# A third buffer for raw weights, and a begin that runs two units side by side on halves of weights, in a fused decoder-layer kernel

## The chip, the cores and the metric

The kernel runs on one core of a Trainium2 chip. The metric is the device time of one launch in microseconds. It is 1373.68 us as the median of three runs (1371.19 to 1373.77).

## The reference, cut to what matters

One inference step of a hybrid decoder layer: 2048 prompt tokens and 32 sample tokens (8 sequences of 4), width 1024, all in float32.

```
h = rmsnorm(x) * norm_g                 # per token
z = h @ w_in                            # 1024 -> 5120: q, f, i, g_a, u, g_b, m_a, m_b
o, S = gated linear recurrence(silu(q), 1 - fgate, i, log fgate), 4 heads of 128, chunks of 32
y_a = (rmsnorm(o) * silu(g_a)) @ w_proj_a
y_b = (group mix(causal means of 2/4/8/16 of u) * scale * silu(g_b)) @ w_proj_b
out = x + (sigmoid(m_a) * y_a + sigmoid(m_b) * y_b) @ w_out
y = rmsnorm(out) * final_norm_g         # outputs: y, the states of both branches
```

## The kernel before, in words

The 2080 tokens are cut into 5 tiles of 416. In each tile the kernel goes through 56 units of weights in a fixed order (`UNITS`): four heads of f, q, i, g; four pairs u, b; the gates ma, mb and the projections y; and eight "out" units. A unit is a 128 x 1024 block of weights, 512 KB, loaded again in every tile. In this text "unit 4" is the fifth, the f of the second head.

Every product is done in three parts for precision. A weight block arrives raw in `wraw`; ScalarE copies it to a rounded high part `whi` (`split`, L807); VectorE subtracts to get the rest, `wlo` (L1061); the input has parts `hhi` and `hlo` likewise. TensorE then does whi x hhi, whi x hlo and wlo x hhi for each of 8 blocks of 128 rows, 24 products a unit (L535 to L537), summed in one of four PSUM banks `Z`. Unit n uses bank n mod 4 as long as no y unit has come, so unit 4 has to wait (`opened`) until the bank of unit 0 has been read.

There are `RAW` = 2 raw buffers and `RING` = 4 buffers for the parts. SyncE loads unit s + 2 at its slot s, once VectorE has made the low part of unit s (L432). ScalarE splits unit s + 3 at its slot s.

Every engine has its own instruction list, written out by hand and worked through in order; they meet by semaphores. Only semaphores and the order within a list set the order of the work.

The begin is special. The input of the first tile isn't normalised before the products: the kernel multiplies with x * norm_g and scales each result afterwards by 1/rms (`xrs0`), in `scale` on VectorE (L1495, L1489). For that, ScalarE squares the 8 blocks (`square`, L1026), VectorE adds them in six steps to two sums (L1530), TensorE adds over partitions with two products of full float32 with ones (`x_squares`, L790), and ScalarE takes logarithm and exponential (`x_norm`, L821, `x_norm_exp`, L825). The ScalarE list does x_norm after the splits of units 3, 4 and 5. TensorE begins with four warm-up products on constant data (`WARM`, L795, two passes each), then `first_unit` (unit 0, in the order in which blocks of the input come), then `late_low` for units 1 and 2 (both products with whi first, those with wlo last; x_squares stands inside unit 2), then the regular units.

After the g of a head (slot 4) VectorE runs that head's chain: decay sums (L1101), factors, keys (L1152), the transpose of the keys to `kt` (L1145, L1147), the split of the next unit and more. SyncE stores `kt` to memory (L497) and reads it back transposed as `ktm` (L506, L508). TensorE takes `ktm` ahead of unit 8 (L591): what stands behind L591 in its list, thus the rest of the kernel, waits for it.

Of the kernel before, what the change touches and what calls it, by code (L numbers as in the profile page):

```python
# [19 lines left out]
F32 = mybir.dt.float32  # L20
# [22 lines left out]
RAW = 2  # L43
# [3 lines left out]
WARM = 4  # L47
# [71 lines left out]
def step_kernel(nc, xT, w_all, consts, w_pool, s_in, buf_in, yT, sp_out, pp_out, ss_out, ps_out):  # L119
    with ExitStack() as ctx:  # L120
# [22 lines left out]
        wraw = [put(f"wraw{i}", [D]) for i in range(RAW)]  # L143
# [78 lines left out]
        vms_at = region(2 * 4 * 4 * P)  # L222
        vms = [put(f"vms{i}", [4, P], F32R, vms_at + 4 * 4 * P * i) for i in range(2)]
        xrs0 = put("xrs0", [T], F32, vms_at)
# [70 lines left out]
        lbe_made = sem("lbe_made")  # L295

# [72 lines left out]
        def raw(t, n):  # L369

            return wraw0[n - RAW] if first(t) and RAW <= n < EARLY else wraw[n % RAW]

        def raw_landed(engine, t, n):
# [3 lines left out]
            elif first(t) and n < EARLY:  # L377
                engine.wait_ge(w0_landed[n - RAW], 16)
            else:
                engine.wait_ge(w_landed[n % RAW], 16 * (t * (NU // RAW) + n // RAW))  # L380
# [23 lines left out]
        def _(sp):  # L404
            for i in range(4):
                sp.dma_start(xin[:, 2 * i:2 * i + 2, :], xT[0, :, 2 * i:2 * i + 2, :]).then_inc(x0_landed[i], 16)
                if i == 0:
                    sp.dma_start(cst[:], consts).then_inc(cst_landed, 16)
                if i == 0:
                    sp.dma_start(wraw[0][:], w_all[0]).then_inc(w_landed[0], 16)  # L410
            sp.dma_start(wraw[1][:], w_all[1]).then_inc(w_landed[1], 16)
# [3 lines left out]
            for n in range(EARLY, FIRST):  # L415
                sp.wait_ge(wlo_made, n - EARLY + 1)
                sp.dma_start(wraw[n % RAW][:], w_all[n]).then_inc(w_landed[n % RAW], 16)
            def tile(t, last):
                for s in range(NU):
# [9 lines left out]
                    if (n < NU or not last) and not (first(t) and n < FIRST):  # L429

                        sp.wait_ge(wlo_made, nth(t, NU, s))
                        sp.dma_start(wraw[n % RAW][:], w_all[n % NU]).then_inc(w_landed[n % RAW], 16)  # L432
# [25 lines left out]
                    if s == 32:  # L458
# [4 lines left out]
                        sp.dma_start(xres[:], xT[t]).then_inc(xres_landed, 16)  # L463
# [67 lines left out]
        def _(pe):  # L531
# [179 lines left out]
            def tile(t, last):  # L711
                for s, (kind, i) in enumerate(UNITS):
# [3 lines left out]
                    if first(t) and s < 3:  # L716
                        if s == 0:
                            first_unit()
                        else:
# [32 lines left out]
            def first_unit():  # L752

                out = Z[0][:, 0:T]
                pe.wait_ge(whi_made, 1)
                for k in range(KD):
                    c = slice(k * P, (k + 1) * P)
                    pe.wait_ge(hhi_made, k + 1)
                    pe.matmul(out, whi[0][:, c], hhi[k][:], start=(k == 0), stop=False)
                    pe.wait_ge(hlo_made, k + 1)  # L760
                    pe.matmul(out, whi[0][:, c], hlo[k][:], start=False, stop=False)
                    if k:
                        first_low(out, k - 1, False)
                first_low(out, KD - 1, True).then_inc(acc_done, 1)

            def late_low(u):
# [3 lines left out]
                for k in range(KD):  # L770
                    if u == 2 and k == 3:
# [9 lines left out]
            def first_low(out, k, final):  # L781
# [947 lines left out]
```

## Time and profile before

| | |
|---|---|
| three runs, median (lowest, highest) | 1373.68 us (1371.19, 1373.77) |
| profiled execution, its own time | 1373.4 us |
| its span, first to last instruction | 1371.7 us |
| TensorE busy | 1358.3 us, 99% of the span |
| VectorE, ScalarE, GpSimdE busy | 933.3, 682.7, 231.2 us |
| mean granted TensorE clock | 0.998 |

The profile is one execution. PE is TensorE's matmul, PEld its weight load, DVE is VectorE, ACT ScalarE, POOL GpSimdE and SPq the queue in which SyncE issues DMAs. Times are counted from the start of the span. A matmul's duration is longer than the step to the next one, as matmuls are pipelined: the step between two starts is what one costs.

### The profile page before, as it was taken

Reading aid. Unit: us, or ns where it says so; the run is one execution under the profiler, and the core shown is the slowest. Engines: PE = TensorE matmul, PEld = TensorE weight load, DVE = VectorE, ACT = ScalarE, POOL = GpSimd, SP = SyncE. Lnnn points to the kernel's source line nnn. Section 1 sums busy time; section 2 is a strip of 40 time slices with the busy share of each in tenths; the row PEclk is TensorE's granted clock in tenths of the full one; section 3 lists DMA queues with packets and bytes.
Section 4 is the critical chain, followed back from the end, with each engine's and each line's share of the span. In section 5 each row is a group of like instructions: output and inputs, shape, how many; then the busy total and the mean of one; then the engine's idle time right before and its main releaser. Section 6 shows DMA issues by size and latency. Waiting matters only on the chain.

```text
span 1371.7 us, 21201 instructions
## 1 busy us (share of the span) xinstructions
PE 1358.3 (99%) x8254; PEld 1342.2 (98%) x8254; DVE 933.3 (68%) x1608; ACT 682.7 (50%) x986; POOL 231.2 (17%) x210
## 2 busy tenths in 40 slices
PE   9999999999999999999999999999999999999997
PEld 7999999999999999999999999999999999999997
DVE  7899555668995456689944566898445589964443
ACT  6565444354674344556633445666334556653332
POOL 2003121120131211101312111012220200130001
PEclk9999999999999999999999999999999999999999
DMA  6544533246545333465363334554533476535329
GB/s 202 145 131 127 208 123 122 94 130 182 135 134 212 119 123 108 132 190 136 109 222 108 123 108 142 170 148 134 195 117 100 137 177 200 178 109 172 119 98 95
DMA packets 140260, 195.92 MB, mean 143 GB/s; under 512 B 83712, under 2 KB 100480, under 8 KB 138496
## 3 DMA queue, kind: packets, MB, share of 16 engines
q1 hardware_dynamic: 140160, 194.56, 47.2%
q8 instruction: 66, 1.08, 0.4%
q14 instruction: 34, 0.28, 0.1%
HBM read 174.91 MB, written 19.61 MB: 142 GB/s over the span
## 4 chain that ended last, share of the span: by engine, by line
PE 81%; DVE 11%; DMA 3%; issue 2%; ACT 2%; SPq 1%; DVEq 0%; ACTq 0%
PE Z L535 25%; PE Z L537 25%; PE Z L536 25%; DVE wlo L1061 2%; DMA wraw<-w_all 1%; DVE h_b L1101 1%; PE B L591 1%; PE B L679 1%; PE B L669 1%; DVE kj L1152 1%; DVE xres L1457 1%; DVE h_d L1111 0%; DVE s_all L1193 0%; DMA xin<-xT 0%; ACT whi L807 0%
## 5 line engine op out<-in xcount | busy, mean ns | idle before, releaser
L1061 DVE TENSOR_TENSOR wlo<-wraw,whi 128x1024 fp32r<-128x1024 f32 x280 | 373.6, 1335 | 308.0 <-ACT whi L807 307.8
L535 PE MATMUL Z<-hhi,whi 128*128 128x416 f32 x1576 | 552.6, 351 | 0.0
L537 PE MATMUL Z<-hhi,wlo 128*128 128x416 f32 x1576 | 549.4, 349 | 0.0
L536 PE MATMUL Z<-hlo,whi 128*128 128x416 f32 x1576 | 549.3, 349 | 0.0
L807 ACT ACTIVATE whi<-wraw 128x1024 fp32r<-128x1024 f32 x280 | 295.6, 1056 | 426.7 <-PE Z L537 336.5
L535 PEld LDWEIGHTS Z<-hhi,whi 128*128 128x128 f32 x1576 | 296.0, 188 | 0.9 <-issue 0.6
L536 PEld LDWEIGHTS Z<-hlo,whi 128*128 128x128 f32 x1576 | 296.0, 188 | 0.5
L537 PEld LDWEIGHTS Z<-hhi,wlo 128*128 128x128 f32 x1576 | 295.8, 188 | 0.2
L537 PE MATMUL Z<-mhi,wlo 128*128 128x416 f32 x320 | 112.3, 351 | 0.0
L536 PE MATMUL Z<-mlo,whi 128*128 128x416 f32 x320 | 111.9, 350 | 0.0
L535 PE MATMUL Z<-mhi,whi 128*128 128x416 f32 x320 | 111.5, 348 | 0.0
L536 PE MATMUL Z<-ylo,whi 128*128 128x416 f32 x320 | 111.4, 348 | 0.0
L537 PE MATMUL Z<-yhi,wlo 128*128 128x416 f32 x320 | 111.4, 348 | 0.0
L535 PE MATMUL Z<-yhi,whi 128*128 128x416 f32 x320 | 111.4, 348 | 0.0
L1619 POOL TENSOR_TENSOR mA<-mA,mB 128x416 f32<-128x416 f32 x40 | 43.5, 1088 | 341.1 <-DVE mB L1264 341.1
L1590 POOL TENSOR_TENSOR pa<-ext 128x430 f32<-128x430 f32 (+1 forms) x20 | 28.0, 1400 | 307.0 <-DVE ext L1493 98.0
L1564 POOL TENSOR_TENSOR yacc<-yacc,ysq 128x416 f32<-128x416 f32 x34 | 37.0, 1088 | 158.4 <-ACT ysq L1014 158.4
L1264 DVE TENSOR_TENSOR mB<-Z,gB 128x416 f32<-128x416 f32 x40 | 23.7, 592 | 58.6 <-PE Z L537 58.3
L1558 POOL TENSOR_TENSOR xacc<-xacc,xsq 128x416 f32<-128x416 f32 x28 | 42.2, 1509 | 113.7 <-ACT xsq L815 113.7
L536 PEld LDWEIGHTS Z<-mlo,whi 128*128 128x128 f32 x320 | 60.1, 188 | 0.6
L535 PEld LDWEIGHTS Z<-mhi,whi 128*128 128x128 f32 x320 | 60.1, 188 | 0.1
L537 PEld LDWEIGHTS Z<-mhi,wlo 128*128 128x128 f32 x320 | 60.1, 188 | 0.0
(249 smaller groups left out, 1613.1 us busy)
## 6 DMA issues: line engine op xcount, KB each, us to landing
wraw<-w_all SPq DMA_DIRECT2D x280, 512.0 KB, 3.5
xres<-xT SPq DMA_DIRECT2D x5, 1664.0 KB, 7.1
xin<-xT SPq DMA_DIRECT2D x4, 1664.0 KB, 7.9
yT<-xres SPq DMA_DIRECT2D x4, 1664.0 KB, 8.5
v_blocks<-h_vt SPq DMA_DIRECT2D x80, 52.0 KB, 3.1
vtm<-v_blocks SPq DMA_DIRECT2D x20, 192.0 KB, 4.0
ktm<-k_blocks SPq DMA_DIRECT2D x20, 192.0 KB, 3.6
k_blocks<-kt SPq DMA_DIRECT2D x64, 52.0 KB, 1.9
```

The source lines that it names most:

```text
L535: pe.matmul(out, wh, xh, start=first, stop=False)
L536: pe.matmul(out, wh, xl, start=False, stop=False)
L537: return pe.matmul(out, wl, xh, start=False, stop=final)
L591: mm = pe.matmul(B6[:, g * P:(g + 1) * P], ktm[:, g, :], vtm[:, g, :], start=True, stop=True)
L669: pe.matmul(B5[:, c], vtm[:, g, :], at_sb[:, c], start=(g == 0), stop=False, skip_group_check=True)
L807: act.activation(whi[n % RING][:], raw(t, n)[:], ACT.Copy).then_inc(whi_made, 1)
L1061: dve.tensor_tensor(wlo[n % RING][:], raw(t, n)[:], whi[n % RING][:].bitcast(F32), ALU.subtract).then_inc(wlo_made, 1)
L1264: dve.tensor_tensor(out[j % 2][:], z_bank(acc, j)[:, 0:T], gate[j % 3][:], ALU.mult).then_inc(z_sem(acc, j), 1)
L1558: pool.tensor_tensor(xacc[:], xacc[:], xsq[k % 2][:], ALU.add).then_inc(xacc_made, 1)
L1564: pool.tensor_tensor(yacc[:], yacc[:], ysq[j % 2][:], ALU.add).then_inc(yacc_made, 1)
L1590: pool.tensor_tensor(wins(level)(first, BUF + n), a, b, ALU.add).then_inc(win_made, 1)
L1619: pool.tensor_tensor(mA[j % 2][:], mA[j % 2][:], mB[j % 2][:], ALU.add).then_inc(merged, 1)
```

## The change

The kernel after has three raw buffers (`RAW` = 3), used in turn across tiles; the third takes the place that `vms` and `xrs0` had, and these move into other buffers. Unit s + 3 is loaded at slot s, still once the low part of unit s is made. In the begin unit 3 has a buffer of its own; unit 4 goes to the buffer of unit 1, and unit 5 to that of unit 2.

The first two units come as halves of 256 KB (columns 0 to 511 and 512 to 1023) between the blocks of the input, and are split in halves. TensorE works on both units side by side, block pair by block pair (`first_pair`). The constants come by ScalarE's own queue. There are three warm-up products in place of four. The squares of the input are added by VectorE in one more step, ahead of the split of unit 2, and x_squares has one product in place of two, behind four blocks of unit 2. VectorE's split of unit 5 moves to slot 2 of the first tile. The load of the residual input is cut in two in the first tile, and `vms` is cleared in the last tile.

```diff
-RAW = 2
+RAW = 3
-WARM = 4
+WARM = 3
...
-            return wraw0[n - RAW] if first(t) and RAW <= n < EARLY else wraw[n % RAW]
+            return wraw0[n - RAW] if first(t) and RAW <= n < EARLY else wraw[(t * NU + n) % RAW]
...
                 if i == 0:
-                    sp.dma_start(cst[:], consts).then_inc(cst_landed, 16)
-                if i == 0:
-                    sp.dma_start(wraw[0][:], w_all[0]).then_inc(w_landed[0], 16)
-            sp.dma_start(wraw[1][:], w_all[1]).then_inc(w_landed[1], 16)
+                    for n in range(2):
+                        sp.dma_start(wraw[n][:, LEFT], w_all[n, :, LEFT]).then_inc(w_half_landed[n], 16)
+                elif i < 3:
+                    sp.dma_start(wraw[i - 1][:, RIGHT], w_all[i - 1, :, RIGHT]).then_inc(w_landed[i - 1], 16)
+            for n in range(2, RAW):
+                sp.dma_start(wraw[n][:], w_all[n]).then_inc(w_landed[n], 16)
...
             for n in range(EARLY, FIRST):
-                sp.wait_ge(wlo_made, n - EARLY + 1)
+                sp.wait_ge(wlo_made, n - RAW + 1)
                 sp.dma_start(wraw[n % RAW][:], w_all[n]).then_inc(w_landed[n % RAW], 16)
...
+            def first_pair():
+                for k in range(0, KD, 2):
+                    if k == 2:
+                        for i in (k, k + 1):
+                            for u in range(2):
+                                high(u, i)
+                                low_weights(u, i)
+                            for u in range(2):
+                                low_input(u, i)
+                        continue
+                    for u in range(2):
+                        for i in (k, k + 1):
+                            high(u, i)
+                            low_input(u, i)
+                        for i in (k, k + 1):
+                            mm = low_weights(u, i)
+                        if k == KD - 2:
+                            mm.then_inc(acc_done, 1)
...
-                    if u == 2 and k == 3:
+                    if k == 4:
                         x_squares()
...
-                for i in range(2):
-                    pe.wait_ge(x0_summed, KD - 3 + i)
-                    mm = pe.matmul(B4[:, 0:T], ones_r[:].bitcast(F32), h0[i][:], start=(i == 0), stop=(i == 1))
-                mm.then_inc(xssq_done, 1)
+                pe.wait_ge(x0_summed, KD - 1)
+                pe.matmul(B4[:, 0:T], ones_r[:].bitcast(F32), h0[0][:], start=True, stop=True).then_inc(xssq_done, 1)
...
+            act.dma_start(cst[:], consts).then_inc(cst_landed, 16)
...
             weighted_hi(0)
             weighted_hi(1)
+            split_half(0, LEFT, w_half_landed, whi_half_made)
+            split_half(1, LEFT, w_half_landed, whi_half_made)
             square(0)
-            split(0, 0)
             weighted_hi(2)
             weighted_hi(3)
-            for k in range(4, KD):
-                weighted_hi(k)
-            split(0, 1)
+            split_half(0, RIGHT, w_landed, whi_made)
+            weighted_hi(4)
+            weighted_hi(5)
+            split_half(1, RIGHT, w_landed, whi_made)
+            weighted_hi(6)
+            weighted_hi(7)
             square(1)
             split(0, 2)
...
+                    if first(t) and s == 2:
+                        split(0, 5)
...
             (VectorE, the begin: hlo 0, 1, left halves, hlo 2, 3, right half of 0, hlo 4, 5, right half of 1, hlo 6, 7)
-            split(0, 1)
-            split(0, 2)
             for k in range(2, KD):
                 dve.wait_ge(xsq_made, k + 1)
                 ...
                 dve.tensor_tensor(h0[k % 2][:], h0[k % 2][:], h0[k][:], ALU.add).then_inc(x0_summed, 1)
+            dve.wait_ge(x0_summed, KD - 2)
+            dve.tensor_tensor(h0[0][:], h0[0][:], h0[1][:], ALU.add).then_inc(x0_summed, 1)
+            split(0, 2)
             split(0, 3)
             bounds()
             split(0, 4)
-            split(0, 5)
```

## Rows read from the trace of the kernel before

**Rows 1.** The page's first part: busy time, share of the span, instructions.
```profile
PE 1358.3 (99%) x8254; PEld 1342.2 (98%) x8254; DVE 933.3 (68%) x1608; ACT 682.7 (50%) x986; POOL 231.2 (17%) x210
```
**Rows 2.** The waits: who waited for whom, us in total, times, longest.
```profile
PE B L591 <- DMA ktm<-k_blocks: 0.4, 2, 0.2
...
ACT whi L807 <- DMA wraw<-w_all: 90.0, 34, 5.8
```
**Rows 3.** The timeline of PE: start, us, line, what, count.
```profile
2.71 5.49 PE L795 MATMUL B<-at_sb,ones_r 128*128 128x384 f32 x8 [2.71 <-DVE ones_r L1466]
8.05 0.47 PE L759 MATMUL Z<-hhi,whi 128*128 128x416 f32 x1
...
18.15 0.35 PE L774 MATMUL Z<-hhi,whi 128*128 128x416 f32 x1
...
19.27 1.56 PE L790 MATMUL B<-h,ones_r 128*128 128x416 f32 x4
...
24.04 0.35 PE L535 MATMUL Z<-hhi,whi 128*128 128x416 f32 x1
...
28.52 0.35 PE L535 MATMUL Z<-hhi,whi 128*128 128x416 f32 x1
```
**Rows 4.** DMA issues of the begin, and the time from issue to landing.
```profile
2.17 1.38 SPq L406 DMA_DIRECT2D xin<-xT  x3
...
DMA to landing us min/median/max: 3.4/6.9/7.8
...
L417 SPq DMA_DIRECT2D wraw<-w_all x1: 328/328/328, 14.5 to 14.5; - x1
...
DMA to landing us min/median/max: 3.5/3.5/3.5
```
**Rows 5.** The timeline of ACT in the begin.
```profile
13.59 1.04 ACT L807 ACTIVATE whi<-wraw 128x1024 fp32r<-128x1024 f32 x1
14.54 2.74 ACT L1026 ACTIVATE h<-xin 128x416 f32<-128x416 f32 x6
...
20.87 0.61 ACT L821 ACTIVATE xrs<-B,eps_t 128x416 f32<-128x416 f32 x1 [0.65 <-PE B L790]
21.51 0.55 ACT L825 ACTIVATE xrs<-xrs 128x416 f32<-128x416 f32 x1
23.78 1.28 ACT L836 ACT_TABLE_LOAD   x1 [1.72 <-DVE Z L1495]
25.07 0.52 ACT L836 ACTIVATE h_sf<-Z 128x416 f32<-128x416 f32 x1
```
**Rows 6.** The timeline of DVE up to the first head's chain.
```profile
9.46 3.47 DVE L1478 SCALAR_TENSOR_TENSOR hlo<-xin,cst,hhi 128x416 fp32r<-128x416 f32 x6 [0.20 <-ACT hhi L1022]
...
15.81 3.10 DVE L1530 TENSOR_TENSOR h<-h,h 128x416 f32<-128x416 f32 x6
18.82 1.22 DVE L1061 TENSOR_TENSOR wlo<-wraw,whi 128x1024 fp32r<-128x1024 f32 x1
...
23.11 0.59 DVE L1495 TENSOR_TENSOR Z<-Z,xrs 128x416 f32<-128x416 f32 x1
...
27.21 0.59 DVE L1093 SCALAR_TENSOR_TENSOR h_qf<-Z,h_qf 128x416 f32<-128x416 f32 x1 [0.58 <-ACT h_qf L836]
...
33.35 1.03 DVE L1101 TENSOR_TENSOR_SCAN h_b<-smask,h_logf 128x416 f32<-128x416 f32 x1 [0.95 <-ACT h_logf L842]
```
**Rows 7.** The keys of the first head, through memory to TensorE, on three engines.
```profile
38.91 0.17 DVE L1147 STREAM_TRANSPOSE kt<-h_e 128x32 f32<-128x32 f32 x1
...
39.11 1.90 SPq L497 DMA_DIRECT2D k_blocks<-kt  x4
...
43.06 0.48 SPq L508 DMA_DIRECT2D ktm<-k_blocks  x1
...
DMA to landing us min/median/max: 3.6/3.6/3.6
...
47.23 0.94 PE L591 MATMUL B<-vtm,ktm 128*128 128x128 f32 x6
```

More of the change, by code:

```diff
@@ L142, in begin_at @@
             top[0] += (offset - top[0]) % 256
-        wraw = [put(f"wraw{i}", [D]) for i in range(RAW)]
+        wraw = [put(f"wraw{i}", [D]) for i in range(RAW - 1)]
         whi = [put(f"whi{i}", [D], F32R) for i in range(RING)]
@@ L221, in step_kernel @@
         vtm = put("vtm", [4, P])
-        vms_at = region(2 * 4 * 4 * P)
-        vms = [put(f"vms{i}", [4, P], F32R, vms_at + 4 * 4 * P * i) for i in range(2)]
-        xrs0 = put("xrs0", [T], F32, vms_at)
+        wraw.append(put(f"wraw{RAW - 1}", [D]))
+        vms = [put(f"vms{i}", [4, P], F32R, y_at + 4 * BS + 4 * 4 * P * i) for i in range(2)]
+        xrs0 = put("xrs0", [T], F32, xr_at + (KD - 1) * B)
         wraw0 = [put(f"wraw0_{i}", [D], F32, xr_at + 4 * D * i) for i in range(EARLY - RAW)]
@@ L379, in raw_landed @@
             else:
-                engine.wait_ge(w_landed[n % RAW], 16 * (t * (NU // RAW) + n // RAW))
+                nth_raw = t * NU + n
+                beside = sum(1 for early in range(RAW, EARLY) if early % RAW == nth_raw % RAW)
+                engine.wait_ge(w_landed[nth_raw % RAW], 16 * (nth_raw // RAW + 1 - beside))
         def s_value(t, last, h, i):
@@ L462, in tile @@
                             sp.wait_ge(y_stored, t * 16)
-                        sp.dma_start(xres[:], xT[t]).then_inc(xres_landed, 16)
+                        ready = KD - 1 if first(t) else KD
+                        sp.dma_start(xres[:, 0:ready, :], xT[t, :, 0:ready, :]).then_inc(xres_landed, 16)
+                    if s == 50 and first(t):
+                        sp.wait_ge(scaled, len(SCALED))
+                        sp.dma_start(xres[:, KD - 1, :], xT[t, :, KD - 1, :]).then_inc(xres_landed, 16)
                 if last:
@@ L717, in tile @@
                         if s == 0:
-                            first_unit()
-                        else:
+                            first_pair()
+                        elif s == 2:
                             late_low(s)
@@ L1293, in tile @@
                         counts()
-                    if s == 50 and first(t):
+                    if s == 2 and last:
                         for v in vms:
@@ L1515, in counts, with split_half @@
                 dve.reciprocal(rc[:], rc[:]).then_inc(rc_used, 1)
+            def split_half(n, c, hi_made, made):
+                dve.wait_ge(hi_made, n + 1)
+                dve.tensor_tensor(wlo[n][:, c], wraw[n][:, c], whi[n][:, c].bitcast(F32), ALU.subtract).then_inc(made, 1)
             weighted_lo(0)
             weighted_lo(1)
-            split(0, 0)
+            split_half(0, LEFT, whi_half_made, wlo_half_made)
+            split_half(1, LEFT, whi_half_made, wlo_half_made)
             weighted_lo(2)
             weighted_lo(3)
-            for k in range(4, KD):
-                weighted_lo(k)
-            split(0, 1)
-            split(0, 2)
+            split_half(0, RIGHT, whi_made, wlo_made)
+            weighted_lo(4)
+            weighted_lo(5)
+            split_half(1, RIGHT, whi_made, wlo_made)
+            weighted_lo(6)
+            weighted_lo(7)
             for k in range(2, KD):
```

34 lines of the change are left out of this document (18 added, 16 removed).

## Prediction

> **What bounds the kernel now.** I read the shares of busy time first: TensorE is busy 1358.3 of 1371.7 us [rows 1], and its work is the same in every execution. So the time can change only by the places where TensorE stands still or works slowly, and by products that go away. Then the waits: behind the begin the largest ones of TensorE are a few tenths, such as those for `ktm`, 0.4 us in two places [rows 2]. ScalarE waits 90.0 us for raw weights, but in another engine's shadow [rows 2]. What is left is the begin, and I went through its timelines engine by engine.
>
> TensorE starts at 2.71 us with the warm-up and begins unit 0 at 8.05; unit 2 begins at 18.15, unit 3 at 24.04 and unit 4 at 28.52 [rows 3]. A product in a regular unit costs (28.52 − 24.04) / 24 = 0.187 us. Units 0 and 1 are 48 products, 8.96 us, and took 10.10, so 1.1 us are lost to waits there. The two products of x_squares are four passes; take the regular 24 products (4.48) from the 5.89 us of unit 2 and they cost 1.41, or 0.70 each. The warm-up's eight passes took at most 8.05 − 2.71 = 5.34, thus 0.67 for 384 columns, where a pass of x_squares takes 0.35 for 416: the warm-up runs at the pace of the lower clock, 1.2 GHz.
>
> **The change, part by part.** *Start of the products.* Six warm-up passes end at 2.71 + 6 x 0.67 = 6.7. The left half of unit 0 is the second DMA. Before, the first input block landed 3.4 us after its issue, by 4.2, and the last 7.8 after its own, by 10.9 [rows 4]; the bytes ahead of it grow from 2190 KB to 2700 KB (four blocks of 416 KB, four halves of 256 KB), which at the pace of the blocks (416 KB a microsecond or so) puts it at 12.1. The first halves should land between 5.4 and 6.9. A half copy on ScalarE costs between 0.46 (a square, [rows 5], 2.74 for 6) and 1.04 (a whole block); I take 0.6. So both engines are ready by about the end of the warm-up, and the first product starts at 6.8, 1.3 us earlier. Some of the first products still run at the lower clock; each such costs 0.16 more. I take three, 0.5 us; the bounds are none and eight (1.3 us).
>
> *The pair.* The last input block limits it: hhi 6 and 7 end at 13.3, hlo 7 by 14.1 (0.57 a step, [rows 6]). The products reach block 6 at 14.0 by their own count (6.8 + 0.5 + 36 x 0.187), so they aren't held up by more than 0.2 us. The pair ends at 16.2 instead of 18.15: 1.9 us are gained here. If nothing followed, this with the product saved in x_squares (0.70) would be the gain, 2.6 us.
>
> *Squares.* ScalarE does unit 2's split at 13.75 (before 13.59) and the squares 2 to 7 until 17.45 [rows 5]. VectorE's six additions, 0.50 apart, run from 15.3 to 18.35, the seventh, added one ends at 19.0. TensorE reaches x_squares at 16.2 + 8 x 0.187 = 17.7 and stands until 19.0: 1.3 us of the gain go. x_squares ends at 19.75, unit 2 at 22.8, unit 3 at 27.3, still 1.25 ahead of before.
>
> *What is late next.* This is the step that I hold to decide. VectorE now makes the low part of unit 2 behind the additions, 18.9 to 20.15 (1.22, as the row at 18.82, [rows 6]); before, that was done before 15.9. The raw weights of unit 5 go into unit 2's buffer and are issued only then, at 20.2. A load issued at 14.5 landed after 3.5 us [rows 4]; with unit 6's load right behind I take 3.6: landed at 23.8. ScalarE's list has the split of unit 5 ahead of x_norm. Its split ends at 24.9, logarithm and exponential take 1.19 (20.87 to 22.06, [rows 5]), and xrs0 is there at 26.0, against 22.06 before. Before, VectorE used it at 23.11 [rows 6], as it was busy with the splits of 4 and 5. The scaling of unit 0 thus starts at 26.05, 2.94 later.
>
> From there two chains go to TensorE. The first is bank 0: scaling 0.6, the table load 1.28, the sigmoid 0.52 [rows 5] free it at 28.5. Unit 4, due at 27.3, begins at 28.6 instead of 28.52 before. So at unit 4 nothing is left of the begin's gain (−0.1 to +0.1).
>
> The second is the keys of the first head. From the scaling at 23.11 to the scan at 33.35 and to `kt` at 39.08 VectorE works nearly without a pause. Moved by 2.94, it also has the split of unit 5 in it now: from scaling to the gated q it took 4.10 us (23.11 to 27.21) with a wait of 0.58 in it; with a split (1.11) in that wait's place 4.55. The chain is 3.4 later. `ktm` landed at 43.06 + 3.6 = 46.7 and was used at 47.23 [rows 7]: 0.5 us to spare. Now it lands at 50.05, while TensorE, with unit 4 at 28.6, stands at L591 from 47.3. It waits 2.8 us, with everything behind it. SyncE's queue in front of this has no new wait: the loads of its slots ask for low parts that are made by 35.
>
> So TensorE is at L591 2.8 to 2.9 us later than before. Lower bound of this term: if unit 5 lands 3.0 us after the issue, and the additions end 0.3 earlier, 1.9; upper bound: 4.4 us to land and 0.4 later squares, 4.1.
>
> *The third buffer later.* It takes ScalarE's 90.0 us of waits away, and makes low parts earlier; at slot 8 of the first tile VectorE gets 2 of its 3.4 us back, so the second head isn't late. TensorE gains only what it waits for: between none and 1.3 us (the few tenths at `ktm`, `vms` and the sums behind the begin). I take 0.4.
>
> *The rest at nothing:* the cleared `vms` (2 x 0.49 us on VectorE) lies in the last tile's slot 2, where VectorE waits over 1.5 us for ScalarE; gone cover would cost at most 1.0 us once. The cut residual load waits for a scaling that is made before its slot, and is used a unit later. The constants' own queue brings them 0.4 earlier, which is under x_squares' wait anyway.
>
> Sum on the profiled execution: 1373.4 + 2.9 − 0.4 = 1375.9; its time is 0.3 below the median shown, so 1376.2 against 1373.68.
>
> A rule beside this: the Trainium skill, DMA: Bandwidth & Descriptors, on the fixed cost, has about 2.0 us for any DMA beside its bytes. By an estimate from it unit 5 would land 3.3 us after its issue (2.0 and 1.3 for its bytes), and the sum would be 0.3 lower.
>
> **Rivals.** *A: the begin's gain is kept.* Mechanism: xrs0 isn't held by unit 5, since its load lands by the time (19.4) at which ScalarE has done its splits of 3 and 4, or little later. Then TensorE's only limits are x_squares and the keys' chain, which would start at x_squares' end + 1.2 = 21.0 or behind VectorE's split of 4 at 23.2, as before. The keys come as before or 0.5 earlier, TensorE can be 0.5 ahead there, and with the later relief the kernel is 0.9 faster: 1372.8. For it speaks that the third buffer makes loads early in all later slots; against it the wait of L417 on the third low part, and the order of VectorE's list. It decides if unit 5 lands before 21.2: then xrs0 is there by 23.5, and the chain of the keys moves by no more than the 0.5 to spare and the 0.4 of later relief. Chance 0.14.
>
> *B: the third buffer gives more later* (all the 1.3 us, and the later heads' chains ahead), with the loss at L591: +1.6, 1375.3. Speaks for it: 34 waits gone. Against: TensorE has hardly a wait to lose. 0.18.
>
> *C: the clock.* With one warm-up product less, and waits among the pair, the products of the pair all run at the 1.2 GHz level. 48 x 0.16 = 7.8 us, the pair ends at 23.5, unit 4 begins at 33.3 and L591 comes 4.8 later than before, past the keys: +4.4, 1378.1. The rows show the warm-up at that level for nearly all its 5.3 us and the first products behind it, from 8.05, at the higher one. 0.06. (The Trainium skill, TensorE: Matmul & The Clock Gate, says the same in its part on the warm-up: it is time under activity, not a number of matmuls, and it varies from run to run. By it the clock rises about where it did, during the first products, and the sum stays.)
>
> **How the numbers follow.** The forecast (0.62) has its own range from 1374.9 to 1377.5. With A below and C above, eight in ten are 1372.8 to 1377.6. What is under 0.2% (2.7 us) can't be told from no change in this kernel. My forecast of +2.5 lies just inside: within 0.2% has nearly 0.6 of the forecast, all of B and most of A, 0.57 in all; slower the rest of the forecast and C, 0.36; faster 0.07, for an A with late waits gone too.
>
> **What would show it.** Right: PE's first product near 6.8; a gap of about 1.3 us ahead of x_squares near 19.0; ACT's split of unit 5 idle before it, on the DMA, until 23.8, and x_norm behind it; unit 4 at 28.6; a wait of over 2 us at L591 for ktm. Wrong: x_norm near 21; L591 at 47 or earlier without a wait; products 0.35 apart beyond 9 us; or a changed sum of waits behind 100 us by more than 1.3 us.

## The result, and the profile after

The changed kernel took 1377.25 us at the median of nine runs (1375.11 to 1378.88), the kernel before, in nine runs beside them, 1373.39 (1371.19 to 1373.88). The ratio is 1.0032, with an interval from 1.0024 to 1.0041: slower, by 3.9 us. The profiled execution of after took 1375.11, that of before 1373.40: the two traces differ by only 1.71 us, the trace of after is that of the shortest of its nine runs, and the other 2.1 us have no trace. Runs 3, 4 and 6 below bear on them. The ratios leave out the few executions of later runs that took far longer (1491 to 3397 us).

The page, parts 1 and 6, against [rows 1, 4]:

```profile
span 1373.4 us, 21216 instructions
PE 1355.6 (99%) x8250; PEld 1342.9 (98%) x8250; DVE 923.4 (67%) x1611; ACT 682.3 (50%) x988; POOL 226.2 (16%) x210
wraw<-w_all SPq DMA_DIRECT2D x278, 512.0 KB, 3.5
ktm<-k_blocks SPq DMA_DIRECT2D x20, 192.0 KB, 3.6
```

TensorE is busy for less time than before and the span is longer, so look for stops. Its waits in after (line, releaser; us in total, times, longest):

```profile
PE Z L547 <- ACT h_sf L861: 2.6, 1, 2.6
PE B L603 <- DMA ktm<-k_blocks: 2.5, 1, 2.5
PE B L816 <- DVE h L1575: 0.5, 1, 0.5
```

The first two are new in this size; before, the read of `ktm` cost 0.4 in two places [rows 2]. L547 is unit 4, which waits until the sigmoid has freed bank 0; L603 is the line that was L591. TensorE's timeline of after gives the places (start, duration, instruction, idle time before it), against [rows 3, 7]:

```profile
6.47 0.46 PE L769 MATMUL Z<-hhi,whi 128*128 128x416 f32 x1
15.72 0.35 PE L806 MATMUL Z<-hhi,whi 128*128 128x416 f32 x1
17.83 0.97 PE L816 MATMUL B<-h,ones_r 128*128 128x416 f32 x2 [0.45 <-DVE h L1575]
21.63 0.35 PE L547 MATMUL Z<-hhi,whi 128*128 128x416 f32 x1
28.88 0.43 PE L547 MATMUL Z<-hhi,whi 128*128 128x416 f32 x1 [2.60 <-ACT h_sf L861]
29.82 0.55 PE L548 MATMUL Z<-hlo,whi 128*128 128x416 f32 x1
...
32.94 0.38 PE L548 MATMUL Z<-hlo,whi 128*128 128x416 f32 x1
...
51.81 0.94 PE L603 MATMUL B<-vtm,ktm 128*128 128x128 f32 x6 [2.48 <-DMA ktm<-k_blocks]
```

Unit 2 starts 2.43 us earlier than before (15.72 against 18.15), unit 3 2.41 earlier. Unit 4 starts 0.36 later than before's 28.52: the whole gain became a wait. Then a second cost, in no table of waits: from 29.82 to 32.94 the products follow each other in 0.35 us instead of 0.187. The windows show why. Their columns are the window, its length, the busy time of each engine, the granted clock, the share of the DMA engines and GB/s:

```profile
28.00:29.00 1.00, 0.12 (x1) 0.15 (x2) 0.23 (x1) 0.72 (x2) 0.65 (x3) 1.00 0.00 0
29.00:30.00 1.00, 1.00 (x5) 0.98 (x6) 1.00 (x3) 0.20 (x1) 0.00 (x0) 0.78 0.00 0
30.00:31.00 1.00, 1.00 (x5) 0.95 (x4) 1.00 (x2) 1.00 (x2) 0.00 (x0) 0.50 0.00 0
31.00:32.00 1.00, 1.00 (x5) 0.95 (x4) 0.96 (x3) 1.00 (x2) 0.00 (x0) 0.50 0.12 25
32.00:33.00 1.00, 1.00 (x5) 0.95 (x4) 1.00 (x4) 0.21 (x1) 0.00 (x0) 0.51 0.74 250
33.00:34.00 1.00, 1.00 (x7) 0.99 (x6) 1.00 (x2) 0.00 (x0) 0.00 (x0) 1.00 0.54 213
```

The clock fell to 0.50 (1.2 GHz) after TensorE had stood still for 2.6 us and had been back at work for some 0.7, and rose at 33. That took the distance to before from +0.36 to +2.0. This loss isn't on the path, though: TensorE came to L603 at 49.3 and waited there for the keys until 51.8. Without the fall it would have come earlier and waited longer, as run 4 shows.

What holds unit 4, and the keys, is seen on ScalarE and VectorE (timelines of after, against [rows 5, 6]):

```profile
16.23 1.99 ACT L832 ACTIVATE whi<-wraw 128x1024 fp32r<-128x1024 f32 x2
24.02 1.06 ACT L832 ACTIVATE whi<-wraw 128x1024 fp32r<-128x1024 f32 x1 [5.80 <-DMA wraw<-w_all]
24.98 0.59 ACT L846 ACTIVATE xrs<-B,eps_t 128x416 f32<-128x416 f32 x1
28.22 0.52 ACT L861 ACTIVATE h_sf<-Z 128x416 f32<-128x416 f32 x1
```

```profile
17.19 0.59 DVE L1575 TENSOR_TENSOR h<-h,h 128x416 f32<-128x416 f32 x1
17.70 2.35 DVE L1095 TENSOR_TENSOR wlo<-wraw,whi 128x1024 fp32r<-128x1024 f32 x2
26.25 0.60 DVE L1531 TENSOR_TENSOR Z<-Z,xrs 128x416 f32<-128x416 f32 x1 [4.18 <-ACT xrs L850]
42.50 0.17 DVE L1181 STREAM_TRANSPOSE kt<-h_e 128x32 f32<-128x32 f32 x1
```

VectorE makes the low part of unit 2 behind the additions, and the load of unit 5 is issued at 18.9. ScalarE stands for 5.80 us until it lands, then splits it, and only then computes the logarithm of x_norm at 24.98, though the product of x_squares had ended at 18.80 (17.83 + 0.97). The two transfers that matter, each as its own issue: the load of unit 5, and the last read of `ktm`, issued at 46.6:

```profile
DMA to landing us min/median/max: 3.6/4.3/5.0
```

```profile
L520 SPq DMA_DIRECT2D ktm<-k_blocks x1: 485/485/485, 46.6 to 46.6; - x1
DMA to landing us min/median/max: 5.1/5.1/5.1
```

In the first fence the line covers units 4 and 5; unit 5 has the 5.0. The read took 5.1 against 3.6 before [rows 7]. So the products of `ktm` began 4.58 us later than before: the read was issued 3.57 us later (46.63 against 43.06) and took 1.58 longer, less the 0.57 us that before had to spare there. From there the loss melts, a few tenths at a time. The starts of the first product behind the same place, in the two traces (worked out by subtracting, before rounding):

| before | after | difference |
|---|---|---|
| 48.15 | 52.73 | +4.58 |
| 76.23 | 80.44 | +4.20 |
| 92.30 | 96.05 | +3.74 |
| 345.77 | 349.09 | +3.31 |
| 614.57 | 617.44 | +2.87 |
| 877.33 | 879.52 | +2.19 |
| 921.01 | 922.73 | +1.72 |

These steps are hardly seen as idle time. At the second row, before has:

```profile
74.18 0.35 PE L537 MATMUL Z<-hhi,wlo 128*128 128x416 f32 x1
74.68 0.91 PE L669 MATMUL B<-at_sb,vtm 128*128 128x128 f32 x6
```

and after, at the same place:

```profile
78.77 0.35 PE L549 MATMUL Z<-hhi,wlo 128*128 128x416 f32 x1
78.96 0.83 PE L681 MATMUL B<-at_sb,vtm 128*128 128x128 f32 x6
```

0.50 us between the two starts before, 0.19 after. Ahead of L669 TensorE's list waits until ScalarE has read the bank that the products go to (`b5_read`). In before ScalarE did that late, behind a split that had waited for raw weights:

```profile
70.53 1.06 ACT L807 ACTIVATE whi<-wraw 128x1024 fp32r<-128x1024 f32 x1 [1.99 <-DMA wraw<-w_all]
73.95 0.59 ACT L866 ACTIVATE h_rst<-B,eps_t 128x416 f32<-128x416 f32 x1
```

The read ended at 74.54. In after it ended 2.4 us ahead of TensorE:

```profile
75.93 0.59 ACT L891 ACTIVATE h_rst<-B,eps_t 128x416 f32<-128x416 f32 x1
```

There are nine such steps of 0.2 to 0.5 us between after and this trace of before, two or three in each of the first four tiles and none in the last. In run 1, which has the third buffer alone, all nine stand at the same places, with the same sizes to 0.01 us. That the cause is the same in the other eight was not followed up.

### The profile page after: what moved, and what is told of

Its sections match the earlier page's. It is cut to its first block, busy times and chain, and to the rows that moved or that the text cites. A ratio compares the mean times of both kernels' runs of the same rounds, so it can differ in the third digit from the quotient of the medians.

```text
span 1373.4 us, 21216 instructions
## 1 busy us (share of the span) xinstructions
PE 1355.6 (99%) x8250; PEld 1342.9 (98%) x8250; DVE 923.4 (67%) x1611; ACT 682.3 (50%) x988; POOL 226.2 (16%) x210
## 3 DMA queue, kind: packets, MB, share of 16 engines
q8 instruction: 66, 1.08, 0.4%
## 4 chain that ended last, share of the span: by engine, by line
PE 89%; DVE 7%; ACT 1%; DMA 1%; issue 1%; SPq 0%; DVEq 0%; ACTq 0%
PE Z L547 28%; PE Z L548 28%; PE Z L549 28%; DVE wlo L1095 1%; PE B L603 1%; PE B L691 1%; PE B L681 1%; DVE xres L1493 1%; PE B L580 0%; DVE snew L1255 0%; DMA xin<-xT 0%; DMA ktm<-k_blocks 0%; DVE h_b L1135 0%; DMA wraw<-w_all 0%; PE B L547 0%
## 5 line engine op out<-in xcount | busy, mean ns | idle before, releaser
L1095 DVE TENSOR_TENSOR wlo<-wraw,whi 128x1024 fp32r<-128x1024 f32 x278 | 363.5, 1308 | 302.7 <-ACT whi L832 302.5
L547 PE MATMUL Z<-hhi,whi 128*128 128x416 f32 x1576 | 553.3, 351 | 2.6 <-ACT h_sf L861 2.6
L547 PEld LDWEIGHTS Z<-hhi,whi 128*128 128x128 f32 x1576 | 296.4, 188 | 3.9 <-issue 3.5
L547 PE MATMUL Z<-mhi,whi 128*128 128x416 f32 x320 | 111.5, 348 | 0.0
L547 PE MATMUL Z<-yhi,whi 128*128 128x416 f32 x320 | 111.4, 348 | 0.0
L547 PEld LDWEIGHTS Z<-mhi,whi 128*128 128x128 f32 x320 | 60.1, 188 | 0.1
```

Source lines behind the costliest of these rows:

```text
L547: pe.matmul(out, wh, xh, start=first, stop=False)
L1095: dve.tensor_tensor(wlo[n % RING][:], raw(t, n)[:], whi[n % RING][:].bitcast(F32), ALU.subtract).then_inc(wlo_made, 1)
```

## The experiments

The kernel before ran beside each group, with medians of 1372.31 (runs 1 to 4), 1372.08 (5 to 8, 11 and 12), 1372.2 (9 and 10) and 1372.43 (13 and 14).

**1. The third buffer alone**, in the kernel before:

```diff
-RAW = 2
+RAW = 3
```

with the places of `vms` and `xrs0`, the count of landings, the waits ahead of the loads of units 4 and 5 and the cut residual load that it needs.

> The kernel before with the third raw buffer alone (its own begin: whole units, four warm-up products, two-product squares). Theory: the buffer takes away the split that waits for raw weights ahead of each head's scores, and gives TensorE the 2.87 us that the kernel after wins between its 73 us and its end; unit 5's load waits for the low part of unit 2, which is made by 15.9 here, so x_norm starts near 20.9 as before and L603 finds ktm landed. Time 1373.4 - 2.9 = 1370.5 (1370.0 to 1371.2). Rival 1, the third buffer brings only few tenths (as forecast) and the later gain belongs to TensorE running late: 1372.5 to 1373.4. Rival 2, the buffer itself makes the loss by loads that run ahead and slow the keys' reads: above 1375.

1370.24 us, ratio 0.9984 [0.9975, 0.9994]. In its trace it is 0.46, then 1.35 (at 346) and at the end 2.95 us ahead of before. By the ratio the buffer is worth 2.2 us (0.8 to 3.4). The forecast gave it 0.4. Run 14 says how far the 2.95 can be trusted.

**2. The begin alone:**

```diff
-RAW = 3
+RAW = 2
```

in after, with the third buffer's place.

> The kernel after with two raw buffers again (side-by-side begin on halves, three warm-up products, squares in one product all kept). Theory: unit 5 loads into unit 1's buffer, waits for its low part (11.8) only, x_norm starts near 19.2, scaling at 22.1; unit 4 starts without a wait near 26.1; the keys come 0.5 to 1.0 earlier than before and cap the gain there; later nothing is won. 1372.4 (1371.6 to 1373.0). Rival (the side-by-side begin itself costs, by the clock or by its order): 1375 or more, with a wait of over 2 us at unit 4 left in the trace.

1380.4 us, 1.0060 [1.0047, 1.0073]. This one misses its own purpose: the loads of units 4 and 5 kept the wait for `n - RAW + 1` low parts, which with two buffers is two too many (3 and 4 where 1 and 2 would do), so they were issued at 19.5 and 20.7. ScalarE waited 6.3 us, unit 4 3.4 us (26.85 to 30.25), and the clock fell while TensorE still stood:

```profile
29.00:30.00 1.00, 0.00 (x0) 0.00 (x0) 0.00 (x0) 0.99 (x2) 0.65 (x4) 0.64 0.17 66
```

(The granted clock is the third figure from the end.) The last read of `ktm` took 5.4 us and TensorE waited 2.8 for it, without a fall behind that. The run shows the same mechanism in a larger size, and not the begin's worth.

**3. x_norm ahead of the split of unit 5** (ScalarE's order alone, the rest is after):

```diff
-            for n in range(3, FIRST):
+            for n in range(3, FIRST - 1):
...
+                    if first(t) and s == 2:
+                        act.wait_ge(acc_done, FIRST - RING)
+                        split(0, FIRST - 1)
```

> The kernel after with ScalarE's split of unit 5 moved behind x_norm, to slot 2 of the first tile. Theory: x_norm near 18.8 instead of 25.0, scaling at 22.1, unit 4 without a wait, L603 waits about 1 us for ktm, the clock stays high, and the 2.9 us of the third buffer come on top of the begin's 1.0: 1369.4 (1368.6 to 1370.4). Rival 1 (the loss is in the keys' way through memory, longer as loads run ahead, 5.1 us to landing in place of 3.6): L603 still waits over 2 us, 1371 to 1373. Rival 2 (the third buffer or the begin costs by itself): above 1374.

1372.61 us, 1.0002 [0.9993, 1.0011]. That is some 4 us faster than after and 3 slower than expected. Unit 4 began at 26.78, without a wait, 1.74 ahead of before; the logarithm stood at 19.51. But then:

```profile
48.34 0.94 PE L603 MATMUL B<-vtm,ktm 128*128 128x128 f32 x6 [2.77 <-DMA ktm<-k_blocks]
```

```profile
50.00:52.00 2.00, 2.00 (x7) 1.92 (x7) 1.89 (x7) 1.10 (x2) 0.00 (x0) 0.50 1.18 289
```

The first fence is TensorE's timeline, the second a window of it. The keys did not come earlier by as much as TensorE did, the read of `ktm` again took long (5.2 us), and the clock fell behind the wait: +1.10 became +2.68. So the wait only moved from unit 4 to L603, and here nothing takes up what the clock costs. The forecast of 1369.4 was missed; the time and the wait are those of the first rival. Of the eleven runs the three with a mean granted clock of 0.998 took 1371.44 to 1371.79 us, the eight with 0.997 took 1372.39 to 1373.90.

**4. TensorE kept busy.** 12 products without use ahead of unit 4, 22 ahead of those of `ktm`:

```diff
+            def filler(n):
+                for _ in range(n):
+                    pe.matmul(B5[:, 0:T], ones_r[:], hhi[0][:], start=True, stop=True)
```

> The kernel after with products that nothing uses in the two waits: 12 of 416 columns ahead of unit 4 and 22 ahead of the products with ktm of the first head; the waits stay, TensorE is busy in them. Theory: the waits' ends are set by the bank of unit 0 and by ktm, so the profile shows unit 4 near 28.9 and L603's line near 51.8 as before, but no granted clock under 1.00 behind unit 4; the time loses what the clock costs in most runs: 1377.25 - 2.1 = 1375.1, with a smaller spread between runs. Rival (the clock has no part in it): 1377.2 and the same spread; or, if the clock's fall near unit 4 is itself on the path, 1373.4.

1375.56 us (1374.91 to 1376.34), 1.0023 [1.0014, 1.0033]. Unit 4 is no earlier (29.01), but the windows have the full clock:

```profile
30.00:32.00 2.00, 2.00 (x13) 2.00 (x12) 2.00 (x3) 2.00 (x3) 0.00 (x0) 1.00 0.00 0
```

TensorE does 13 products in the two microseconds where after does 10, and comes to the place of `ktm` at 47.8, 1.5 us earlier than in after. It gains nothing there: the keys land at 51.4, and the 22 products reach a little beyond that, so that the products of `ktm` start at 52.08 against 51.81 in after. The profiled executions are alike, 1375.24 and 1375.11. So the fall seen at unit 4 costs after's trace nothing.

The gain is in the runs without a trace: 1.2 us by the ratios, whose intervals overlap, and 1.7 by the medians. The mean granted clock, which each run has, points at the clock: in after the five shortest runs have 0.997 (1375.11 to 1377.25), the four longest 0.996 (1377.60 to 1378.88); here nine of eleven have 0.998, the others 0.997. In runs 3 and 6 the runs part in the same way. A further fall behind L603, as run 3's trace has it, would be on the path and would fit. The mean doesn't say where the clock fell, and in its last digit it isn't sharp (run 7's trace has 0.997 without a fall inside), so this stays argued. The spread alone proves nothing: the runs lie within 1.4 us here and within 3.8 in after, but those of before within 2.7, and in its trace the clock doesn't fall between the begin and its last products.

**5. The begin alone, loads early:** two buffers in after, and the wait mended.

```diff
-                sp.wait_ge(wlo_made, n - RAW + 1)
+                sp.wait_ge(wlo_made, n - EARLY + 1)
```

> As the second experiment (the new begin with two raw buffers), but unit 4 and unit 5 are loaded once the low parts of unit 0 and unit 1 are made, as the kernel before does; the second experiment had asked for two more, which put both loads behind 19.5 us. Theory: x_norm near 19.5, unit 4 near 26.8 without a wait; ktm is issued near 43.1 and lands 5.2 us later, as TensorE's fetch of 16 KB of instructions near 45.5 falls on it; L591's line waits 2.8 us and the clock falls for 3.4 us behind it: +2.3 at unit 10, nothing given back later: 1374.7, 1.5 to 3 above before. Rival (the side-by-side begin is sound and the third buffer brings the trouble): 0.5 to 1 faster than before.

1376.74 us, 1.0030 [1.0018, 1.0041]. Unit 4 began at 26.72, but the keys were stored 1.4 us later than in run 3 (40.51 against 39.15), since ScalarE's splits waited for raw weights; `ktm` landed 5.4 us after its issue, and TensorE waited

```profile
PE B L602 <- DMA ktm<-k_blocks: 4.4, 1, 4.4
```

in which the clock fell, and it stayed low until 55:

```profile
48.00:49.00 1.00, 0.00 (x0) 0.00 (x0) 1.00 (x3) 0.18 (x1) 0.00 (x0) 0.59 0.86 337
```

The forecast of 1374.7 was too low by 2. With two buffers the earlier begin is a loss, by the slow read and the clock.

**6. The keys' way made shorter:** run 3, and VectorE scales unit 0 ahead of the bounds and of the split of unit 4.

```diff
+            dve.wait_ge(xrs_made, 1)
+            scale(*UNITS[0])
...
```

> The kernel of the third experiment with VectorE's scaling of unit 0 ahead of the bounds and of the split of unit 4 (ScalarE asks for the bounds at slot 2 only). Theory: the scaling starts near 20.75 instead of 22.66, the chain of the first head's keys comes 1.9 earlier, kt near 37.2, ktm lands near 44.7 ahead of TensorE (45.5) and of its instruction fetch; no wait of over 0.3 us, no fall of the clock, the begin's 1.7 us stay and the third buffer's 2.9 come on top: 4.3 faster than before, 1368 to 1369.2. Rival (VectorE's chain isn't what sets the keys; the path through memory is): L603 still waits 1.5 us or more, within 1 us of the third experiment (1371.6 to 1372.6).

1372.15 us, 0.9996 [0.9987, 1.0005]. The stores of the keys were issued 0.9 us earlier than in run 3 (38.21 against 39.15), and the wait fell to 2.3:

```profile
47.19 0.94 PE L603 MATMUL B<-vtm,ktm 128*128 128x128 f32 x6 [2.27 <-DMA ktm<-k_blocks]
...
49.32 0.35 PE L547 MATMUL Z<-hhi,whi 128*128 128x416 f32 x1
49.88 0.35 PE L547 MATMUL Z<-hhi,whi 128*128 128x416 f32 x1
```

From one of these rows of L547 to the next are three steps, 0.56 us: the clock stayed high. The profiled run took 1370.54, but the median is no better than in run 3 by anything that can be told: the forecast of 1368 to 1369.2 failed, and time and wait are those of the rival. The eleven runs fall in two groups: four with a mean granted clock of 0.998 took 1370.29 to 1371.01 us, the profiled one among them, and seven with 0.997 took 1372.03 to 1373.41. So the same kernel likely has the clock fall in some runs and not in others, and its trace is one without a fall.

**7. The low part of unit 2 ahead of the additions**, with after's order on ScalarE kept. It tests the forecast's own chain: if the late load of unit 5 is the cause, moving one instruction must take the loss away.

```diff
+            split(0, 2)
...
-            split(0, 2)
```

> The kernel after with VectorE's split of unit 2 ahead of the additions, as before; ScalarE's order untouched (x_norm behind the split of unit 5). Theory: unit 5 is issued near 14.8 instead of 18.9 and lands by 19.5; x_squares waits 1.1 us longer (to 19.0), x_norm starts near 20.0 instead of 25.0; unit 4 starts without a wait near 27.4. At L603 the state is that of the third experiment (a wait for ktm of 2 to 3 us with the clock's fall): 1372.6 to 1373.4, 4 us faster than after. Rival (the late x_norm comes from something else than unit 5's load): 1376 or more, ScalarE still waits over 4 us ahead of x_norm.

1370.8 us, 0.9986 [0.9977, 0.9995]. TensorE's waits:

```profile
PE B L816 <- DVE h L1576: 1.6, 1, 1.6
PE B L603 <- DMA ktm<-k_blocks: 1.4, 1, 1.4
```

and ScalarE's x_norm without a wait for weights ahead of it:

```profile
17.27 3.17 ACT L832 ACTIVATE whi<-wraw 128x1024 fp32r<-128x1024 f32 x3
20.57 0.61 ACT L846 ACTIVATE xrs<-B,eps_t 128x416 f32<-128x416 f32 x1
```

x_squares waits 1.1 us longer than in after, unit 5 is issued at 15.9 and is there in time, unit 4 starts at 27.84 and no clock falls there. At unit 8 it is 0.79 behind before instead of 4.58. This is the cleanest test of the cause: one instruction moved by seven places on VectorE makes 6.4 us by the medians (6.3 by the ratios), of which the two traces have 3.7. The forecast of 1372.6 to 1373.4 was too high, as the wait at L603 was 1.4 and not 2 to 3 us. The slow read of `ktm` is in this run too (5.0 us), so that read alone doesn't make the kernel slower than before.

**8. The slow read of `ktm`.** In runs 2, 3 and 5 to 7 as in after the last read took 5.0 to 5.4 us, in before and run 1 3.55. In the slow ones an engine's fetch of instructions, 16 KB in one packet, starts 2.1 to 2.9 us behind the issue. It is seen as a queue of its own in the DMA view of such a stretch, here after from 48.9 to 50.2:

```profile
DMA packets 213, 0.17 MB, mean 127 GB/s; under 512 B 26, under 2 KB 197, under 8 KB 212
q8 instruction: 1, 0.02, 5.0%
```

5.0% of 16 engines in 1.3 us is one DMA engine taken for 1.04 us. To move the fetch, run 3 got 20 products of 32 columns ahead of unit 4:

```diff
+                    if first(t) and s == 4:
+                        for _ in range(20):
+                            pe.matmul(B5[:, 0:CHUNK], ones_r[:], hhi[0][:, 0:CHUNK], start=True, stop=True)
```

> The kernel of the third experiment with 20 products of 32 columns ahead of unit 4 that nothing uses: 40 more instructions on TensorE for about 1.5 us of its time, where it has 2.8 us to spare at ktm. Theory: its fetch of instructions comes 3 us earlier, near 42, ahead of the reads of ktm; the last of them lands after 3.6 us, near 46.7; L603 starts there with hardly a wait, the clock stays: 2.5 to 2.8 faster than the third experiment, about 1369.8. Rival (ktm is slow by contention with the weights, the fetch has no part): still 5 us to landing, and the same time as the third experiment or up to 0.3 more.

1371.0 us, 0.9991 [0.9981, 1.0000]: 1.6 faster than run 3, where 2.5 to 2.8 was forecast. The fetch came at 41.57 and lengthened a store of the keys to 4.1 us, but the read landed 2.15 us after its issue; TensorE waited 0.6, and the clock stayed.

**9. Both, with the fetch ahead of the keys:** run 6 and 20 small products ahead of x_squares.

```diff
+                        for _ in range(20):
+                            pe.matmul(B5[0:CHUNK, 0:CHUNK], ones_r[:, 0:CHUNK].bitcast(F32),
+                                      hhi[0][:, 0:CHUNK].bitcast(F32), start=True, stop=True)
```

> The sixth experiment's kernel with 20 products of 32 x 32 (two passes each, 80 instructions, about 0.7 us) that nothing uses, in TensorE's wait ahead of x_squares. Theory: the fetch of instructions that fell at 44.42 and made the last read of ktm land after 5.0 us comes 7 us earlier, ahead of the stores of kt (38.2); the read lands after 3.6 us at 45.7, TensorE waits 0.8 us there instead of 2.3 and the clock stays in all runs: L603 near 45.8 against 47.23 before, the third buffer's 2.9 on top: 4.4 faster than before, 1367.7 (1367.3 to 1368.8). Rival (the long landing comes from the weights' loads beside it): still 5 us to landing, and 1371.5 to 1372.5 as the sixth.

1369.46 us (1368.95 to 1370.01), 0.9979 [0.9970, 0.9988]: faster than both kernels, 2.7 us less than before (by the ratio 2.9) and 7.8 less than after (by the ratios 7.3). The fetch was at 36.2, the read took 3.5, and the products of `ktm` had no wait. The forecast of 1367.7 was missed by 1.8. The load of unit 5 says the same as the read: in after and runs 3, 4, 6 and 8 a fetch started 1.7 to 2.0 us behind its issue and it landed after 5.0 to 5.1 us; here the fetch came before the issue and it landed after 3.5, in run 12 after 3.4. The list of TensorE's waits holds no line of the begin but the warm-up's:

```profile
PE B L823 <- DVE ones_r L1508: 2.7, 1, 2.7
PE B L666 <- ACT ysq L1026: 0.4, 1, 0.4
PE B L641 <- DVE vms L1415: 0.4, 1, 0.4
```

**10, 11 and 13. The fetch on the read in the kernel before**, with 2, 4 and 6 small products ahead of its x_squares, to slow the read there on purpose.

> The kernel before with two products of 32 x 32 (8 instructions, under 0.1 us) that nothing uses ahead of x_squares. Theory: its fetch of instructions moves from 45.97 to about 45.2 and so onto the last read of ktm, issued at 43.1: that lands after 5.0 to 5.2 us, near 48.1, TensorE waits 0.8 us at L591 and the kernel is 0.8 to 1.0 slower than before. Rival (fetches don't slow the read): 3.6 us to landing, no wait, a time within 0.2 of before.

> As the tenth experiment, with four products of 32 x 32 (16 instructions, 0.15 us) ahead of x_squares: there the fetch fell 2.73 us behind the issue of the last read of ktm and missed it. Theory: it comes 1.5 us earlier than in the kernel before, about 2.0 us behind the issue, and makes the read land after 5.0 to 5.4 us; TensorE waits 0.8 to 1.5 us at L591; 1.0 to 1.5 slower than before. Rival (fetches don't slow the read): 3.6 us to landing, no wait, within 0.3 of before.

> As the tenth experiment, with six products of 32 x 32 (24 instructions, 0.3 us) ahead of x_squares. Theory: the fetch comes between 43.6 and 45.0, 1 to 2.3 us behind the issue of the last read of ktm (42.9), which lands after 5.0 us or more; TensorE waits 0.6 to 1.2 us at L591; about 1.2 slower than before. Rival (fetches don't slow the read): 3.6 us to landing, no wait for it, 0 to 0.3 slower.

1371.7, 1373.34 and 1372.84 us; 0.9999 [0.9990, 1.0008], 1.0009 [0.9999, 1.0018], 1.0006 [0.9997, 1.0015]. The read landed after 3.58, 3.67 and 3.68 us: no slow read. But the fetch started 2.73, 2.83 and 2.86 us behind the issue in all three, wherever the products were meant to push it. In before and run 1 it is 2.9, so it had hardly moved against the read, and the forecasts of a slow read failed. In run 7 it was 2.87 behind, and that read took 5.0. The other five slow reads had it 2.1 to 2.6 behind. So runs 8 and 9 and the load of unit 5 speak for the fetch, these three show that its distance alone doesn't settle it, and the cause of the slow read stays open.

**12. Four warm-up products instead of three**, in run 9's kernel.

```diff
-WARM = 3
+WARM = 4
```

> The ninth experiment's kernel with four warm-up products in place of three. Theory: the warm-up ends 0.6 to 1.3 us later, the first product starts near 7.1 to 7.6 and the pair ends later by as much; the wait ahead of x_squares (taken up by the small products there) gives nothing back, so unit 4 starts 0.6 to 1.2 later and L603 with it: 0.6 to 1.2 slower than the ninth: 1370.1 to 1370.7. Rival (the low input parts of the last blocks set the pair's end anyway): no difference.

1369.7 us, 0.9983 [0.9974, 0.9992]. The first product is at 6.89 instead of 6.30 and unit 4 0.57 later, and the profiled executions differ by 0.55 (1369.51 and 1368.96); by the medians and ratios the times can't be told apart.

**14. The kernel before again**, unchanged, for a second trace.

> The kernel before, unchanged, for a second trace. If the first trace was a slow one, the products behind 73 us stand 1 to 2 us earlier in this one against their first of unit 10, with no change in the code; the third buffer's share is then 1 to 2 us in place of 2.9. If the 2.9 all belong to the third buffer, this trace agrees with the first to 0.5 us at the last product.

1373.63 us, 1.0005 [0.9995, 1.0014]. Its trace is 0.46 ahead of the first at unit 4 and 0.57 behind it at 921: the first trace of before was no outlier. The traces of the two-buffer kernel (this one, and runs 10, 11 and 13) lie from 1.8 us ahead of the first to 0.6 behind it at that place. This bears on the third buffer's worth. From 48.15 to 921, after and runs 1, 4, 6, 7, 9 and 12 each gain 2.9 us on the first trace of before (run 3, with the clock's fall in it, 1.3, and run 8 2.2). But runs 10, 11 and 13, with two buffers, gain 1.9, 0.7 and 2.1 on it as well, and this run loses 1.0. Against the mean of the five traces that have before's two buffers and its begin the third buffer is worth 2.1 us, which agrees with what run 1 measured (2.2).

## Why the prediction was wrong

The mechanism stood: by the chain from VectorE's late low part over the load of unit 5 and x_norm, to bank 0 and to the keys, the kernel lost its begin and more. Run 7 cuts that chain at its first link and the loss is gone. What failed is the size, and with it the likeliest side: 1376.2 was forecast and 1377.25 came, inside the range, but the loss is 3.9 us (0.24 to 0.41% by the interval of the ratio, 3.3 to 5.6 us) and not 2.5, past the 0.2% that I held likeliest. The step that failed is the price of TensorE's lateness at L603. The forecast had +2.9 there, from a read of `ktm` of 3.6 us and from a wait that costs its length and nothing more; the clock behind the waits was put at nothing. The runs showed +4.58, with a read of 5.1 us, and behind such a wait a fall of the clock worth 1.6 (run 3) that after's runs without a trace likely have. The other large miss, the third buffer at −0.4 for −2.2, went the other way: had that term alone been right, the forecast would have been +0.7. So it is in part luck that 1377.25 lies inside the range. The steps:

- *Start of the products*, 6.8: it was 6.47, and at the high clock at once. The three slow products weren't there in this trace; in runs 2, 3, 4 and 6, with the same warm-up, three to five products stood 0.35 apart. The pair ended at 15.72, not 16.2; the last input block landed at 11.0, not 12.1.
- *x_squares waits 1.3 until 19.0*: it waited 0.45 until 17.83, as the additions began at 14.05 rather than 15.3. Unit 3 was 2.4 us ahead, not 1.25. So the begin gained more than I said, and lost it in the same place: unit 4 at 28.88 (forecast 28.6).
- *Unit 5 issued at 20.2, landed after 3.6*: issued at 18.9, landed after 5.0. Two errors that cancel; 23.94 for 23.8. A fetch of instructions began at 20.6, in this load too (see run 9). x_norm, scaling (26.25 for 26.05) and the last transpose of the keys (42.50 for 42.5) followed as forecast. The estimate by the Trainium skill, DMA: Bandwidth & Descriptors, on the fixed cost (fitted there to DMAs that GpSimdE issues, while SyncE issues this one), would have had the load after 3.3 us; the trace says 5.0, and the trace decides. By the rate that the Trainium skill has in the same place the bytes take 1.2 us, and not the 1.3 of the prediction.
- *The wait at unit 4.* I worked it out as a time at which TensorE starts again and gave it no cost but its length. With the larger gain ahead of it, it grew to 2.6 us, and the clock fell behind it: TensorE lost 1.6 us, which the wait for `ktm` then took up. The clock was left out of the wait at L603 too, and there a fall is on the path, as in run 3. Rival C had a low clock, but in the pair, where there was none.
- *The read of `ktm`, the term at L603*: 3.6 was taken from before, 5.1 came. Of the 4.58 us at L603 this is 1.5. The forecast 2.9 and this 1.5 make 4.4; the rest, 0.2, is the later issue. That TensorE would wait 2.8 came near (2.48), since the slow products had used up part of the lateness.
- *The third buffer later*, −0.4: it is −2.9 against the first trace of before, −2.1 against the mean of the five and −2.2 timed in run 1. Rival B's size (1.3) was nearer, and still short. I summed TensorE's listed waits; what was given back stands in no list, as the 0.31 us that went from between the starts of two products above. ScalarE's waits for raw weights were not all in another engine's shadow.
- *The sum.* +4.6 − 2.9 = +1.7 is what the two profiled executions have. The medians have 3.9. The 2.1 us between are likely in good part the clock in the other runs (runs 3, 4 and 6), and that is argued, not shown. Another part may be the begin: additions on VectorE that end at 17.78 in after end at 18.45 in run 3, which has the same work up to there.
- *Small slips of the working*: the scaling to the gated q with a split is 4.10 − 0.58 + 1.11 = 4.63, not 4.55; rival C's 48 x 0.16 is 7.7, not 7.8; and the chances listed for a change within 0.2% add up to about 0.6, not 0.57. None decides anything.

That x_norm would not wait (rival A) was false for after, but run 3 made it true: it gained 4 us on after and none on before, as the keys, the read of `ktm` and the clock took the place of the wait. The "cleared vms" and the residual load cost nothing, as forecast: L641, the products of `vms`, waits 0.4 in after as in runs 1 and 4 (L640, L647) and in before (L629).

## What to carry to other kernels

When the begin is pulled forward, ask which load is issued behind the work that was moved ahead: a chain of four engines hung here on one subtraction, placed behind seven additions. Price a wait of TensorE of over two microseconds with and without a fall of the clock (here 1.6 us where it fell behind a wait of 2.6 to 2.8), and not by its length only; then ask whether a later wait takes that up, as L603 did for unit 4. One trace shows one of the cases: compare the granted clocks of all runs. And a stretch in which no wait is listed can hold tenths between the starts of two products in each head: compare the starts of equal instructions in two traces before calling a buffer worthless.

## What the runs showed of the hardware

- The granted clock can fall behind a wait of TensorE or inside it, and the length of the wait doesn't settle whether it does. It fell to 0.50 some 0.7 us behind a wait of 2.6 (unit 4 of after), 1.4 us behind one of 2.77 (run 3), and inside waits of 3.4 (run 2) and 4.4 us (run 5); behind 2.8 (L602 of run 2), 2.48 (L603 of after) and 2.27 (run 6) it stayed at 1.00. The fall cost TensorE 1.6 us each in after and in run 3. The Trainium skill, TensorE: Matmul & The Clock Gate, in its part on the warm-up, calls the start of the clock variable from run to run. For the start the traces agree (by the steps between products the rise is in the warm-up of after, and behind the first products in runs 2, 3, 4 and 6), and the two groups of run 6, 0.998 and 0.997, say as much for a fall.
- Instructions are fetched by DMA, through the same 16 engines as the data. The trace of after has 66 packets on queue row 8 with 1.08 MB, 16 KB each, and one of them takes one engine for about 1 us. Products added on TensorE moved them (runs 8 and 9). Reads that took 5.0 to 5.4 us had such a fetch 2.1 to 2.9 us behind their issue, six times out of six; but three reads with it at 2.7 to 2.9 took 3.6 to 3.7, as did those of before and run 1 with it at 2.9. The relation is not settled.
- Three warm-up products were enough for the high clock from the first real one, at 6.47 us, in after; in runs 2, 3, 4 and 6 they weren't.
